# Four moves in a fused two-block kernel: convolution taps, a narrower short convolution, key swaps, and the turning of row tile 1

## What is computed

```
z = rms_norm([meta, x]) @ w_in
conformer: z = a * sigmoid(gate); z = causal_dwconv(z, w_dw) + b      # 31 taps, 256 channels
short:     y = bg * causal_dwconv(cg * xv, w)                         # 3 taps, 256 channels
return h_res[:, 16:]                                                  # the meta rows are dropped
...
q, k, v = split(x @ moba_w_in); q = partial_rope(q); k = partial_rope(k)   # 32 of 128 dims per head
o = softmax(q k^T * scale, causal) @ v                                # 8 heads, one block of 256 keys
x = layer_norm(ALPHA * x + o @ w_out);  x = layer_norm(ALPHA * x + swiglu(x))
```

## Time and profile before

| | us |
|---|---|
| median of 3 runs | 901.54 |
| lowest, highest | 901.53, 903.14 |
| the profiled execution, its own time | 904.15 |
| its span, first to last instruction | 902.4 |
| PE busy | 880.3 (98%) |
| DVE, ACT, POOL busy | 594.7, 425.7, 128.1 |

### The profile page before, as it was taken

The page is one execution under the profiler, slowest core; times in us unless marked ns, Lnnn a source line. Parts: engine busy times, 40 slices in busy tenths (PEclk is TensorE's granted clock), DMA queues, the critical chain, the costliest instruction groups (busy, mean ns, idle before and its releaser), DMA issues.

```text
span 902.4 us, 14004 instructions
## 1 busy us (share of the span) xinstructions
PE 880.3 (98%) x5895; PEld 801.7 (89%) x5895; DVE 594.7 (66%) x825; ACT 425.7 (47%) x608; POOL 128.1 (14%) x114
## 2 busy tenths in 40 slices
PE   9999998999999999999999999997999999999996
PEld 7997998998888988879999988787987899999884
DVE  5997995687586584786555554675876765555535
ACT  5645453456654874435444443254544464444420
POOL 0342530121101311011000000025320200000000
PEclk9999999999999999999999999998999999999999
DMA  8753664663354852447655555374542765555531
GB/s 302 235 176 91 190 186 139 185 184 119 96 163 140 256 164 94 146 155 236 187 187 187 186 187 188 122 262 139 155 146 90 225 218 186 185 187 182 189 123 47
DMA packets 116008, 154.18 MB, mean 171 GB/s; under 512 B 5391, under 2 KB 91818, under 8 KB 115914
## 3 DMA queue, kind: packets, MB, share of 16 engines
q1 hardware_dynamic: 114218, 148.31, 51.6%
q0 software_dynamic: 1728, 4.98, 1.7%
HBM read 151.44 MB, written 1.05 MB: 169 GB/s over the span
## 4 chain that ended last, share of the span: by engine, by line
PE 89%; DVE 9%; issue 1%; ACT 1%; DVEq 0%; POOL 0%; POOLq 0%
PE acc L578 25%; PE acc L579 25%; PE acc L580 25%; DVE w_lo L1574 2%; DVE conv L1715 2%; PE acc L649 1%; PE acc L646 1%; PE acc L647 1%; DVE y L1994 1%; PE misc L738 1%; PE misc L791 1%; PE misc L729 1%; PE acc L616 1%; DVE sc_acc L1735 1%; PE misc L973 1%
## 5 line engine op out<-in xcount | busy, mean ns | idle before, releaser
L1574 DVE TENSOR_TENSOR w_lo<-staged,w_hi 128x1024 fp32r<-128x1024 f32 (+1 forms) x274 | 336.7, 1251 | 162.2 <-ACT w_hi L1163 161.7
L578 PE MATMUL acc<-x_hi,w_hi 128*128 128x256 f32 (+1 forms) x1288 | 367.9, 286 | 3.0 <-DVE m L1794 3.0
L579 PE MATMUL acc<-x_lo,w_hi 128*128 128x256 f32 (+1 forms) x1288 | 365.5, 284 | 0.0
L580 PE MATMUL acc<-x_hi,w_lo 128*128 128x256 f32 (+1 forms) x1288 | 363.1, 282 | 0.0
L1163 ACT CAST w_hi<-staged 128x1024 fp32r<-128x1024 f32 (+1 forms) x274 | 278.0, 1045 | 86.2 <-DMA staged<-in_ffn_w_down 45.9
L578 PEld LDWEIGHTS acc<-x_hi,w_hi 128*128 128x128 f32 x1288 | 243.6, 189 | 5.8 <-DVE m L1794 3.2
L580 PEld LDWEIGHTS acc<-x_hi,w_lo 128*128 128x128 f32 x1288 | 245.4, 191 | 0.0
L579 PEld LDWEIGHTS acc<-x_lo,w_hi 128*128 128x128 f32 x1288 | 243.9, 189 | 0.7 <-issue 0.2
L578 PE MATMUL acc<-w_hi,h_hi 128*128 128x512 f32 x176 | 69.7, 396 | 0.0
L580 PE MATMUL acc<-w_hi,h_lo 128*128 128x512 f32 x176 | 69.6, 396 | 0.0
L579 PE MATMUL acc<-w_lo,h_hi 128*128 128x512 f32 x176 | 69.6, 395 | 0.0
(11 more groups left out here) (375 smaller groups left out, 1183.8 us busy)
## 6 DMA issues: line engine op xcount, KB each, us to landing
staged<-in_ffn_w_gu SPq DMA_DIRECT2D x88, 512.0 KB, 3.5
staged<-in_w_in SPq DMA_DIRECT2D x58, 512.0 KB, 3.5
staged<-in_ffn_w_down SPq DMA_DIRECT2D x44, 512.0 KB, 3.5
staged<-in_gla_w_in SPq DMA_DIRECT2D x24, 512.0 KB, 3.9
staged<-in_moba_w_in SPq DMA_DIRECT2D x24, 512.0 KB, 4.7
staged<-in_w_o SPq DMA_DIRECT2D x8, 512.0 KB, 3.8
staged<-in_gla_w_out SPq DMA_DIRECT2D x8, 512.0 KB, 3.6
staged<-in_moba_w_out SPq DMA_DIRECT2D x8, 512.0 KB, 3.7
```

The costliest lines, as they stand in the source:

```text
L578: pe.matmul(dst, st_hi, mv_hi, start=start, stop=False)
L579: pe.matmul(dst, st_hi, mv_lo, start=False, stop=False)
L580: return pe.matmul(dst, st_lo, mv_hi, start=False, stop=stop)
L1574: nc.vector.tensor_tensor(lo, raw, hi, ALU.subtract).then_inc(split, 1)
```

## The change

Four parts, all by hand-written order:

1. The short convolution's inputs are projected for 258 columns (the 256 rows and the two before them) in slots 10 to 13; ACT's copies and POOL's product are cut to the same columns.
2. Seven taps instead of one stand in DVE's z slot 17; then one tap each in slots 18, 20, 21, 23, 25 and in gate_sc's slots 1 to 7.
3. In MoBA, POOL issues the swap of pair j's keys right behind the swap of its queries, ahead of the queries' rotation.
4. In the four tails tile 1 is turned behind tile 0's whole pass, in pieces of 2, 2 and 4 transposes (5 bank uses for each tail instead of 4); the last piece stands inside tile 1's pass with x_hi, behind its first quarter.

The eight matmuls on x_lo now stand together, and tile 1's first matmul stands right behind the transposes that make its operand. The core of the diff:

```diff
-Z_TAPS.update({17: (12, 13), 18: (13, 14), 20: (14, 15), 21: (15, 16), 23: (16, 17), 25: (17, 19)})
+Z_TAPS.update({17: (12, 19), 18: (19, 20), 20: (20, 21), 21: (21, 22), 23: (22, 23), 25: (23, 24)})
...
-                elif sl.index <= 6:
-                    conv_taps(17 + 2 * sl.index, 19 + 2 * sl.index)
+                else:
+                    conv_taps(23 + sl.index, 24 + sl.index)
...
+            xs_hi, xs_lo = x_hi[:, :, META - SC_K + 1:KEYS], x_lo[:, :, META - SC_K + 1:KEYS]
...
-            z(6, 14)
+            z(6, 10)
+            t_stage(10, 4, 5, xs_hi, xs_lo)
...
+TURNED = [(0, 0, 4), (0, 4, 4), (1, 0, 2), (1, 2, 2), (1, 4, 4)]
...
-                            if part == 0:
-                                pe.wait_ge(s["x_rounded"], done + 2 * t + j + 1)
-                            elif t == 0:
-                                if j == 1:
-                                    turn_rows(tag, 2)
...
+                                u = j if t == 0 else 2 + min(q, 2)
+                                if part == 0:
+                                    pe.wait_ge(s["x_rounded"], 5 * turn + u + 1)
+                                    if t == 1 and q == 1:
+                                        turn_rows(tag, 4)
...
                     if t == 0:
+                        turn_rows(tag, 2)
                         turn_rows(tag, 3)
...
             for j in range(4):
                 swap_halves("q", mq, mq_swap, j)
+                swap_halves("k", mk, mk_swap, j)
                 pool.wait_ge(s["swapped_q%d" % j], 32)
                 rotate(mq, mq_swap, r32, j, mrope_pool, trig[r32, 0, :], trig[r32, 1, :], s["mq_roped"], j + 1)
-                swap_halves("k", mk, mk_swap, j)
```

More of the change, by code:

```diff
@@ L107 @@
     MISC += ["mt%d" % _h for _h in range(HEADS) if SCORES_AT[_h] + 2 == _n]
-MISC += ["x4_%d" % _i for _i in range(4)] + ["gt1_0", "gt1_1"]
+MISC += ["x4_%d" % _i for _i in range(5)] + ["gt1_0", "gt1_1"]
 TAIL_OUTS = {_n: (_n + _s + "0", _n + _s + "1") for _n, _s in (("gla_out", ""), ("down0", "_"), ("moba_out", ""), ("down1", "_"))}
@@ L624, in n_first @@
                 open_out(name)
-                done = 4 * (int(tag[1]) - 1)
+                turn = int(tag[1]) - 1
                 for t in range(TILES):
@@ L629, in n_first @@
                         for j in range(2):
-                            if part == 0:
-                                pe.wait_ge(s["x_rounded"], done + 2 * t + j + 1)
-                            elif t == 0:
-                                if j == 1:
-                                    turn_rows(tag, 2)
-                                pe.wait_ge(s["x_rest"], done // 2 + j + 1)
-                            else:
-                                await_read(pe, "%s_%d" % (tag, 2 + j))
-                            for q in (2 * j, 2 * j + 1):
+                            if part == 1 and t == 0:
+                                pe.wait_ge(s["x_rest"], 2 * turn + j + 1)
+                            for q in (2 * j, 2 * j + 1):
+                                u = j if t == 0 else 2 + min(q, 2)
[3 more added lines that the diff above has]
+                                        turn_rows(tag, 4)
+                                elif t == 1:
+                                    await_read(pe, "%s_%d" % (tag, u))
                                 sl = Slot(FIRST[stage] + q, q)
@@ L1939, in rest_rows @@
             def rest_rows(tag, u):
-                t, j = u // 2, u % 2
-                dve.wait_ge(s["x_rounded"], 4 * (int(tag[1]) - 1) + u + 1)
-                read(rest(x_lo[:, 4 * j:4 * j + 4, t * P:t * P + P], bank("%s_%d" % (tag, u))
-                          .rearrange("p (c r) -> p c r", c=4), x_hi[:, 4 * j:4 * j + 4, t * P:t * P + P]), "%s_%d" % (tag, u))
+                t, lo, n = TURNED[u]
+                name = "%s_%d" % (tag, u)
+                dve.wait_ge(s["x_rounded"], 5 * (int(tag[1]) - 1) + u + 1)
+                read(rest(x_lo[:, lo:lo + n, t * P:t * P + P], bank(name)[:, 0:n * P].rearrange("p (c r) -> p c r", c=n),
+                          x_hi[:, lo:lo + n, t * P:t * P + P]), name)
             dve.wait_ge(s["gain_scaled"], 1)
```

39 lines of the change are left out of this document (22 added, 17 removed).

## The result

The changed kernel takes 893.0 us (median of four, 892.59 to 894.22) where the kernel before took 902.3 beside it (901.53 to 903.38): the ratio is 0.9901, with a 95% interval of 0.9885 to 0.9917. The prediction was 889.3 with a range of 886.5 to 894.0, so the sign and the range held, and the gain is 9.3 us where the sum gave 12.3.

A forecast was written before the change was run, and what follows sets the result against it. PE, busy 98% of its span, was taken as the bound. Terms 0.56 + 2.7 + 1.54 + 4.2 + 2.43 + 0.85 = 12.3 us came off the median 901.54, giving 889.3, range 886.5 to 894.

The forecast's parts named there:

- Taps: Taps moved behind slot 17: 2.7 us of PE's wait for m and 1.54 us of lower clock go, minus 4.2 us.
- The cover: Around slot 18: weights are split 6 slots ahead, some 17 us, so DVE's delay of 1.8 reaches PE nowhere else.
- each DVE instruction that meets one loses 1.05 us: Behind slot 17: a moved tap's DVE instruction running beside one of POOL's 12 rotating instructions loses 1.05 us.
- The delay that I had put at 1.8: DVE's delay around slot 18 from six taps moved in and three more meetings with POOL: 1.8 us, bounds 0.8 and 2.9.
- Columns: Slots 10 to 13 at 258 columns: 96 matmuls on PE's path each save about 6 ns, 0.56 us.
- Tails: Tile 1 turned behind tile 0's pass: 0.45 us saved in each of x2 to x4, 0.5 lost in x1, together 0.85.
- MoBA: Keys' swap first: wait before the first scores 1.2 us instead of 5.4, and 2.43 us of lower clock gone, minus 6.6.
- For pair 1 the keys' slot ends 3.5 us after the first scores: MoBA pair 1: q's rotation behind POOL's new wait ends at 630.5, PE wants q near 634, so nothing is late.
- A: Rival: at MoBA DVE and POOL block each other more, PE idles 2.5 us, the clock falls as before: 893.0; chance 0.13.
- B: Rival: taps meet POOL at full price, DVE 2.9 us late or more, PE idles 1.5, clock falls: 891.9; chance 0.09.
- C: Rival: PE reads slots 10 to 13 slower from column 14, 96 x 0.30 = 29 us, so 918; chance 0.02.
- D: Rival: keys' swap issued early lands no earlier, sharing the queue with q's two DMAs; MoBA stall stays: 895.9; chance 0.03.

The follow-up runs named there:

- the quiet kernel: The changed kernel with the keys' swap issued ahead of q's rotation for pair 0 only, pairs 1 to 3 in the old order: 890.93 us, ratio 0.9875.

## Why the prediction came out as it did

**Taps: the gain right, the way to it in part wrong.** The cover, the 2.93 us of the tap beside POOL in slot 18 and the end of the stall are as forecast. A rest of 0.35 us was forecast and there is none: PE was taken to come 0.56 earlier by the columns while DVE stayed, but DVE moves with it. What failed is the step "each DVE instruction that meets one loses 1.05 us", applied to the taps moved in. Not one of them lost anything; POOL did, and it handed the delay on to two of DVE's `sc_acc` instructions some 17 us later (0.9 us each, while slot 18's w_lo gained 0.7). The delay that I had put at 1.8 is 1.2 (from slot 18's w_lo to slot 20's, 104.72 less 87.64 before, 104.81 less 86.54 after), and the taps gone ahead of m are worth 4.7 and not 5.05. With the common shift of start and columns, 1.1, that gives the 4.6 us by which the first instruction for m starts earlier. That 1.8 lay near is luck.

The forecast gain of this part, 2.7 + 1.54 = 4.24, was read from one execution in which the clock fell. Measured alone on the kernel before it is 3.6, on the quiet kernel 5.4. The forecast lies between. That a short idle leaves the clock alone was read from the earlier trace rows, whose window ends at 402.00, 0.12 us before PE resumes; the two windows behind it (402 to 406) are at 1.00 too, so the reading holds.

**Columns: right.** 0.55 to 0.57 in the profiles, 0.68 by the times. Nothing shows that a start at column 14 costs anything.

**Tails: right in sum and sign by sign.** 0.85 was forecast, 0.64 is in the profile, 0.76 in the times. x1 lost 0.54 where 0.5 was forecast; x2 to x4 gained 0.4 where I had 0.45. The two casts of 256 columns took 0.65 together, and PE waits 0.24 of it.

**MoBA: the second step that failed, and the one that cost time.** For pair 0 the step was right and even on the careful side: 7.2 us for 6.6, the wait left is 0.7 and not 1.2, and the clock does not fall. Two of DVE's three rotating instructions were blocked (1.49 and 1.77 us), the third was not (0.68). Unblocked the three would take 2.0 us; they took 3.9. By the Trainium skill, page "SBUF — State Buffer", section "Who interferes with whom", VectorE with both inputs in SBUF and GpSimd share one port pair, and while one of them holds it the other is blocked. The trace agrees in that one of the two is held up, here and at pair 1 (there in the two w_lo, and in the norm's instructions too, which have one tensor input); that they take turns, as the prediction has it, does not hold at slot 17, where five taps went by while POOL's first instruction stood. What failed is the sentence "For pair 1 the keys' slot ends 3.5 us after the first scores ... Nothing is late next there". It asked whether q would be late, behind POOL's new wait, and q is not: it is done at 626.57. It did not ask beside whom q's rotation would then run. It runs beside DVE's norm and the two w_lo right ahead of the keys, and the keys come 1.1 us late, at pairs 1 and 2. I had named POOL and DVE as blocking each other at slot 18 and at pair 0 and left it out at pair 1. The kernel with the early swap in pair 0 alone shows the cause, and its size: 2.2 us. The prediction had put "a new wait of over 1 us stands elsewhere" among the signs that it is wrong, and there are two.

**The sum.** Between the two profiles the gain is 11.3 us where 12.3 was forecast: MoBA gave 1.6 less (5.0 for 6.63), the tails 0.2 less, the wait for m 0.3 more, and 0.5 came from the start, which the prediction did not have and which is no part of the change. The other 2.0 of the 3.0 missing in the medians (9.3 for 12.3) come from the choice of the execution that the sum was formed from. The profiled execution of before, at 904.15, is 1.8 us slower than the median of its runs, 902.34, and that of after is 0.2 faster than its own. In the slow one both stalls were followed by a lower clock and the first scores waited 5.4 us. That is not what an execution of before costs on the mean: they range from 897.5 to 904.9, and the profiles show two reasons, the clock, which stayed up behind m in one of five executions with a stall of 3 us, and the wait before the scores, which was 3.4, 4.5, 5.4, 5.4 and 5.6 us. To take the whole difference off the median was the error of size; the interval of the measurement is 1.4 us to either side. (That the median came out at 893.0 and not 889.3 has 0.8 us more from the median of before itself, 901.54 over three runs and 902.34 over four.) The lower bound also holds a slip: it takes 2.7 for the clock behind MoBA's stall where the working has 2.43. By that it would be 886.8.

**Rivals.** A (the MoBA stall only shortened to 2.5 and the clock falls) gives the right time, 893.0, by the wrong way: the waits sum to 3.0, but in three pieces, and the clock is at 1.00. B falls: DVE was 1.2 us late, not 2.9, and PE never waited. (What B rests on is so, the tap of slot 18 still takes 2.93; the delay that it draws from it did not come.) C falls: slots 10 to 13 take 11.47 us for 96 matmuls, 0.1195 each. D falls in its main point: the early swap lands early. Yet with q's swap issued 3.8 us ahead of it (602.80) DVE started on it 4.3 us after its issue, 4.9 in the kernel with the early swap in pair 0 alone, where the earlier trace rows show 4.0.

## What to carry to other kernels

Moving a wait forward in an in-order queue moves all that stands behind it: ask for each moved instruction not only who waits for it, but which engine it will now run beside, and once per round of the loop, since round 0 and round 1 need not have the same neighbours. Having no neighbour isn't needed. In the faster kernel here q's rotation still meets DVE; it only no longer meets the instructions right ahead of what PE waits for. A reorder that pays in the first round only should be made there only. A stall whose price differs from execution to execution is priced by the median of several, not by the profiled one. Where a kernel's executions spread by 5 us because of a stall, measure half-microsecond parts on the version without the stall, by leaving each part out.

## What the runs showed of the hardware

The lower clock behind an idle stretch is not a function of its length alone. Stalls of 3.02, 3.02, 2.98 and 2.98 us before the same matmul were followed by it (0.50 at the lowest), one of 2.99 was not. Stalls of 3.4 to 5.6 us before MoBA's scores were followed by it in all five profiles. Ones of 0.7 to 1.1 us in the midst of the program never were, nor one of 1.43, but one of 1.11 us, 12 us after the start, was, while 1.23 us there was not. A fall costs time on top of the idling. Behind m, 60 matmuls took 8.5, 8.7, 8.7 and 9.8 us where they took 7.23 without it: 1.3 to 2.6 more. Between MoBA's first two scores it was 5.1 to 6.3 us for 3.58: 1.5 to 2.7 more.

The mean clock of an execution goes with its time, also where there is no profile. In the kernel with the keys' part alone, where the only long stall is the one of 3 us for m, the 12 executions lie in groups at 0.998, 0.996 and 0.993 to 0.994, with medians 897.3, 899.0 and 900.1 us: no fall, it seems, and two lengths of it. Executions with a mean clock of 0.997 still differ by up to 1.4 us, so it does not explain all of the spread.

The keys' swap, two transfers of 16 partitions each, was there for DVE 4.0, 4.0, 3.5, 3.1 and 2.4 us after POOL began to issue it (the kernel before, tails alone, taps alone, the old order in the changed kernel, columns alone), with nothing changed in the swap itself; issued 3.2 to 4.2 us behind q's swap, in the early order, it took 4.3 to 4.9 in the eight profiles where DVE waited for it.

The rotation instructions of POOL on 32 partitions of 512 take 1.28 us alone and up to 2.35 beside DVE, and 3.14 beside the run of taps. Of DVE's instructions beside POOL each blocked one loses 0.8 to 1.1 us whatever its own length: 0.29 and 0.35 become 1.11 and 1.40 (tensor-scalar), 0.68 becomes 1.49 and 1.77 (rotation), 0.69 becomes 1.59 and 1.65 (`sc_acc`). So short instructions suffer most. But not every one that overlaps is blocked: the five taps beside POOL's 3.14 us took 0.41 each, and it was POOL that lost 1.9 us. Which of the two is held up is not settled here.
